# Attention inputs of the last block as tokens x features, with 512-column weights as the moving operand

## The chip, the cores and the metric

The program runs on one core of one Trainium2 chip. The metric is the device time of one execution in microseconds (us).

## What is computed

The reference runs two blocks one after the other on 256 tokens of 1024 features (the first with 16 meta tokens in front). The change lies in the second block, and there in what follows the one wide projection `proj = h @ w_in`:

```python
proj = h @ w_in[l]
(q_a, k_a, v_a, q_i, k_i, w_i, q_b, k_b, v_b, gate_a, gate_b) = jnp.split(proj, split_at, axis=-1)
q_a = apply_rope(rms_norm_2(q_a.reshape(B, S, DSA_HEADS, HEAD_DIM_2), g_q_dsa[l]), cos_h, sin_h)
k_a = apply_rope(rms_norm_2(k_a.reshape(B, S, DSA_HEADS, HEAD_DIM_2), g_k_dsa[l]), cos_h, sin_h)
...
score = jnp.einsum('bqh,bqhs->bqs', wib.astype(jnp.float32), jax.nn.relu(logits))
_, sel = lax.top_k(score, topk)
...
def rms_norm_2(x, gain):
    xf = x.astype(jnp.float32)
    y = xf * lax.rsqrt(jnp.mean(xf * xf, axis=-1, keepdims=True) + EPS)
    return (y * gain.astype(jnp.float32)).astype(x.dtype)

def apply_rope(x, cos, sin):
    x1, x2 = jnp.split(x.astype(jnp.float32), 2, axis=-1)
    return jnp.concatenate([x1 * cos - x2 * sin, x2 * cos + x1 * sin], axis=-1).astype(x.dtype)
```

The queries and keys of both attentions (4 heads of 128 features each) are normalised per token and head and rotated. The first attention (`_a`) keeps for each token the 64 keys of the best index score; the second (`_b`) is causal over the one block of 256.

## The kernel before

All matrix products are of float32 quality in three passes: a weight unit is split by ACT (ScalarE) into a rounded high part `w_hi` (L1741) and by DVE (VectorE) into the rest `w_lo` (L983, or in halves of 1024 columns by `low_half`, L1003), and PE (TensorE) forms high x high, high x low and low x high (L363 to L365) into the same PSUM bank. Weights come in units of 1 MB, 128 x 2048 numbers, through a ring of four slots. SP fetches a unit as soon as DVE is done with the slot's old one; ACT waits until PE has used up the old high part (`weights_used`, or `tile_done` at the end of a group).

Everything is held as features x tokens: the 128x128 piece of a weight is the stationary operand, and the 256 tokens of x move. The stage `w_in` has one small unit (index key and head weights) and eleven groups of 512 features, two units each: group 0 is the index queries `qi`, then `v_a`, `q_a`, `k_a`, `v_b`, `q_b`, `k_b`, and groups 7 to 10 are the gates. A group is 4 tiles x 8 input tiles x 3 passes, 96 products of 256 columns, into four of the eight banks. DVE copies the tiles out (`evict4`, L1328) and frees the banks (`tile_evicted`).

The order of every engine is written out by hand. PE runs group after group, and after each of the eight input tiles of a group a table `between` can put other work (`group`, L385):

- `turn_v`: four 128x128 transposes into bank 7 turn half of the values into tokens x features (L859).
- `qk_sums`: the squares of a head group, which ACT has made (`qk_squares`, L2020), are summed over the features by eight products with a column of ones (L651). ACT takes the root (L2025), DVE the reciprocal (L1378).
- `qk_spread`: eight products spread the reciprocals over 128 partitions (L663), twice per group, and DVE multiplies by them and by the gain (`qk_norm`, L1556).
- `qk_rotate`: a product with a signed permutation in plain float32 (L832), twice per group, and three DVE operations apply cosine and sine (`rotation`, L1509 to L1518).
- `idx_scores` (L850), `scores2` (L888, L890), `turn_p2` (L903) and `values2` (L916) are the index scores and the attention itself; the four steps of the first attention stand in groups 5 and 6, those of the second in groups 8 and 9.

All that use bank 7 wait in `bank7_free` for the last reader of it. Between them DVE finds the 64 best index scores in eight rounds of maximum and replacement for each half of the tokens (`take_best`, L1541, L1542), then writes the selection mask (`select`). `scores2` waits for it. The last group is followed by `br_dsa`.

The lines that give the shape of a product and of what stands between:

```python
ins = three_pass(ps[:, st.bank(t), 0:st.cols], u % RING, (kk * GROUP + m) * P,
                 xs[0][:, k, 0:st.cols], xs[1][:, k, 0:st.cols], k == 0, k == KT - 1)
...
def qk_jobs(name):
    return {0: [lambda: qk_sums()], 2: [lambda: qk_spread(0)], 3: [lambda: qk_spread(1)],
            4: [lambda: qk_rotate(name, 0)], 5: [lambda: qk_rotate(name, 1)]}
...
group(w_in, 3, xs, between=qk_jobs("q_a"))
group(w_in, 4, xs, between=qk_jobs("k_a"))
```

Of the kernel before, what the change touches and what calls it, by code (L numbers as in the profile page):

```python
# [24 lines left out]
ALU = mybir.AluOpType  # L25
# [42 lines left out]
N_SHIFTED = 190  # L68


class Stage:


    def __init__(self, plan, name, units, tiles, tokens, k_outer, quad_banks=False, tail=False):
# [32 lines left out]
    def evicted(self, t):  # L107

        return t - self.e_shift

# [5 lines left out]
def build(nc, w_units, mod_units, x_in, vectors, constants, tables2, out):  # L116
    ctx = ExitStack()
    with ctx:
# [27 lines left out]
        stage("w_in", "w_in", 23, 48, SEQ, False, True)  # L146
# [52 lines left out]
        v2_T = at("v2_T", 12 * KB, [P, 4, SEQ])  # L199
        qi = at("qi", 28 * KB, [P, 4, SEQ])  # L200
        gates = at("gates", 32 * KB, [P, 16, SEQ])
        work1 = at("work1", 48 * KB, [P, 4, SEQ])
        work2 = at("work2", 52 * KB, [P, 4, SEQ])
        tab = at("tab", 56 * KB, [P, 4, SEQ])
# [24 lines left out]
        def norm_part(name, offset, shape, dt=F32):  # L229
# [17 lines left out]
        eps = sb("eps", [P, 3])  # L247
# [31 lines left out]
            "scored", "max_ready", "probs_ready", "weights_ready", "p_turned", "pT_ready", "pv_done", "o_evicted",  # L279
            "idx_scored", "idx_relu", "idx_used", "sel_ready", "gate_ready",  # L280
# [18 lines left out]
        V_GROUP2 = (1, 4)  # L299
# [57 lines left out]
        def _(pe):  # L357
# [14 lines left out]
            def wait_bank(st, t, shift=0):  # L372
# [7 lines left out]
                elif st.name == "w_in" and t < st.t0 + 3 * GROUP:  # L380
                    n = st.evicted(st.t0 + GROUP)
                pe.wait_ge(S["tile_evicted"], n + shift)

            def group(st, g, xs, i=0, x_base=None, bank_busy=None, between=None):

                for half in range(2):
                    u = st.u0 + 2 * g + half + (1 if st.name == "w_in" else 0)
                    pe.wait_ge(S["lo_ready"], u + 1 + 4 * i)
                    for kk in range(4):
                        k = 4 * half + kk  # L390
                        hi_first = x_base is not None and k == 0 and st.u0 > 0
                        if hi_first:
                            pe.wait_ge(S["x_hi_ready"], x_base + 1)
                            for m in range(GROUP):
                                t = st.t0 + GROUP * g + m + (4 if st.name == "w_in" else 0)
# [6 lines left out]
                        if hi_first:  # L402
                            for m in range(GROUP):
                                t = st.t0 + GROUP * g + m + (4 if st.name == "w_in" else 0)
                                pe.matmul(ps[:, st.bank(t), 0:st.cols], w_hi[:, u % RING, m * P:m * P + P],
                                          xs[1][:, 0, 0:st.cols], start=False, stop=False)
                        for m in range(0 if not hi_first else GROUP, GROUP):
                            t = st.t0 + GROUP * g + m + (4 if st.name == "w_in" else 0)
# [403 lines left out]
            def bank7_free():  # L812

                for name, n in (("v_stored", c.now("turned")), ("rotation_read", c.now("rotated")),
                                ("head_std", c.now("head_sums")), ("normed_heads", c.now("head_spread") - 4),
                                ("o_evicted", c.now("pv_done"))):
# [3 lines left out]
            def key_and_weights():  # L820
# [6 lines left out]
                c.up("rotated")  # L827
# [26 lines left out]
            def turn_v(g, kt):  # L854

                bank7_free()
                pe.wait_ge(S["tile_evicted"], w_in.evicted(w_in.t0 + GROUP * (V_GROUP2[g] + 2)))
                for m in range(4):
                    ins = pe.transpose(ps[:, 7, m * P:(m + 1) * P], v2_T[:, m, kt * P:(kt + 1) * P], ident)  # L859
                ins.then_inc(S["turned"], 1)  # L860
                c.up("turned")
# [1399 lines left out]
```

## Time and profile before

| | |
|---|---|
| median of 3 runs | 1532.84 us (1532.22 to 1532.97) |
| profiled execution | 1531.38 us |
| its span | 1529.5 us |
| PE / weight loads busy | 1474.2 us (96%) / 1443.6 us (94%) |
| DVE / ACT busy | 1065.0 us (70%) / 680.7 us (45%) |
| mean granted clock of PE | 0.994 |
| read from HBM | 266.73 MB, 175 GB/s |

The span is what the profile shows of the execution; the execution's own time holds about 2 us more. The busy time of PE counts overlapping products once, so 96% says that something was always in the array, not that it ran at its best rate. How fast products follow each other is read from their starting times in the timeline.

### The profile page before, as it was taken

How to read it: one execution, taken by the hardware profiler on the slowest of the kernel's cores; microseconds unless marked ns; L12 is line 12 of the kernel's file. 1: busy time of each engine (PE TensorE's matmuls, PEld its weight loads, DVE VectorE, ACT ScalarE, POOL GpSimd, SP SyncE). 2: the span in 40 equal slices, each digit the busy share in tenths (PEclk: the TensorE clock that was granted, in tenths of full speed). 3: DMA queues.
4: the chain of work that ended last, by engine and by line, in shares of the span. 5: the costliest groups of instructions: out<-in, count | busy, mean ns of one | idle time of the engine just before them, and what ended most of it. 6: DMA issues, size and time to landing. Idle time of an engine off the chain costs nothing. (4 is left out here: it accounts for less than half of the span.)

```text
span 1529.5 us, 29328 instructions
## 1 busy us (share of the span) xinstructions
PE 1474.2 (96%) x12027; PEld 1443.6 (94%) x12027; DVE 1065.0 (70%) x1443; ACT 680.7 (45%) x809; POOL 28.9 (2%) x58
## 2 busy tenths in 40 slices
PE   5999999999999999999999979999999999999999
PEld 4999999999999999999988879999898989999999
DVE  5666878776667876677867676668877665776653
ACT  5443344354443454433545555443432535454441
POOL 0000100000000000000000000001000000000000
PEclk9999999999999999999999989999999999999999
DMA  7545745436447555457332135558343234454550
GB/s 295 188 166 191 262 179 193 165 105 244 174 165 251 217 193 184 173 196 286 141 131 107 60 138 193 201 187 302 149 142 134 84 117 179 173 188 170 176 209 29
DMA packets 41677, 269.14 MB, mean 176 GB/s; under 512 B 4672, under 2 KB 5824, under 8 KB 12272
## 3 DMA queue, kind: packets, MB, share of 16 engines
q1 hardware_dynamic: 33120, 240.31, 43.6%
q0 software_dynamic: 7312, 26.44, 4.9%
q8 instruction: 71, 1.16, 0.3%
q10 hardware_dynamic: 1152, 1.05, 0.2%
q14 instruction: 22, 0.18, 0.0%
HBM read 266.73 MB, written 1.05 MB: 175 GB/s over the span
## 5 line engine op out<-in xcount | busy, mean ns | idle before, releaser
L363 PE MATMUL ps<-x_hi,w_hi 128*128 128x272 f32 (+2 forms) x2488 | 725.1, 291 | 29.6 <-DVE w_lo L983 16.5
L364 PE MATMUL ps<-x_lo,w_hi 128*128 128x272 f32 (+2 forms) x2488 | 708.6, 285 | 0.0
L365 PE MATMUL ps<-x_hi,w_lo 128*128 128x272 f32 (+2 forms) x2488 | 708.5, 285 | 0.0
L1741 ACT ACTIVATE w_hi<-raw_weights 128x2048 fp32r<-128x2048 f32 x222 | 423.5, 1912 | 362.7 <-PE ps L365 362.5
L983 DVE TENSOR_TENSOR w_lo<-raw_weights,w_hi 128x2048 fp32r<-128x2048 f32 x196 | 447.1, 2290 | 167.3 <-ACT w_hi L1741 166.7
L363 PEld LDWEIGHTS ps<-x_hi,w_hi 128*128 128x128 f32 x2488 | 472.6, 190 | 37.8 <-DVE w_lo L983 16.5
L364 PEld LDWEIGHTS ps<-x_lo,w_hi 128*128 128x128 f32 x2488 | 473.0, 190 | 2.8 <-issue 2.4
L365 PEld LDWEIGHTS ps<-x_hi,w_lo 128*128 128x128 f32 x2488 | 472.5, 190 | 0.0
L363 PE MATMUL ps<-a_hi,w_hi 128*128 128x272 f32 x592 | 169.6, 286 | 0.0
L364 PE MATMUL ps<-a_lo,w_hi 128*128 128x272 f32 x592 | 169.6, 286 | 0.0
L365 PE MATMUL ps<-a_hi,w_lo 128*128 128x272 f32 x592 | 169.6, 286 | 0.0
L363 PE MATMUL ps<-a_hi_s,w_hi 128*128 128x256 f32 x416 | 116.1, 279 | 1.3 <-DVE o L1384 0.8
L364 PE MATMUL ps<-a_lo_s,w_hi 128*128 128x256 f32 x416 | 115.0, 276 | 0.0
L365 PE MATMUL ps<-a_hi_s,w_lo 128*128 128x256 f32 x416 | 115.0, 276 | 0.0
L363 PEld LDWEIGHTS ps<-a_hi,w_hi 128*128 128x128 f32 x592 | 111.5, 188 | 0.0
L364 PEld LDWEIGHTS ps<-a_lo,w_hi 128*128 128x128 f32 x592 | 111.5, 188 | 0.0
L365 PEld LDWEIGHTS ps<-a_hi,w_lo 128*128 128x128 f32 x592 | 111.5, 188 | 0.0
L1768 ACT ACTIVATE pair_a<-pair_a 128x544 f32<-128x544 f32 (+1 forms) x44 | 28.7, 653 | 168.5 <-DVE pair_a L1026 168.5
L363 PEld LDWEIGHTS ps<-a_hi_s,w_hi 128*128 128x128 f32 x416 | 78.2, 188 | 1.8 <-DVE o L1384 1.0
L1003 DVE TENSOR_TENSOR w_lo<-raw_weights,w_hi 128x1024 fp32r<-128x1024 f32 (+1 forms) x71 | 77.9, 1111 | 2.4 <-ACT w_hi L1741 1.9
L364 PEld LDWEIGHTS ps<-a_lo_s,w_hi 128*128 128x128 f32 x416 | 78.2, 188 | 0.1
L365 PEld LDWEIGHTS ps<-a_hi_s,w_lo 128*128 128x128 f32 x416 | 78.2, 188 | 0.0
(247 smaller groups left out, 1375.2 us busy)
## 6 DMA issues: line engine op xcount, KB each, us to landing
raw_weights<-w_units SPq DMA_DIRECT2D x228, 1024.0 KB, 4.9
mod_w<-mod_units POOLq DMA_DIRECT2D x48, 512.0 KB, 5.3
h<-x_in SPq DMA_DIRECT2D x1, 1088.0 KB, 5.5
out<-h ACTq DMA_DIRECT2D x8, 128.0 KB, 1.9
tab<-tables POOLq DMA_DIRECT2D x1, 512.0 KB, 10.0
tab<-constants POOLq DMA_DIRECT2D x1, 272.0 KB, 3.1
con<-constants POOLq DMA_DIRECT2D x2, 128.0 KB, 6.6
f<-constants POOLq DMA_DIRECT2D x1, 136.0 KB, 7.0
```

Of the source, the lines that this page charges most:

```text
L363: pe.matmul(dst, wh, hi, start=start, stop=False)
L364: pe.matmul(dst, wh, lo, start=False, stop=False)
L365: return pe.matmul(dst, wl, hi, start=False, stop=stop)
L983: dve.tensor_tensor(w_lo[:, u % RING, :], raw[:, u % RING, :], w_hi[:, u % RING, :].bitcast(F32), ALU.subtract).then_inc(S["lo_ready"], 1)
L1003: ins = dve.tensor_tensor(w_lo[:, u % RING, cols], raw[:, u % RING, cols], w_hi[:, u % RING, cols].bitcast(F32), ALU.subtract)
L1741: act.activation(w_hi[:, u % RING, :], raw[:, u % RING, :], ACT.Copy).then_inc(S["hi_ready"], 1)
L1768: act.activation(pair_a[:, :, 0:T], pair_a[:, :, 0:T], ACT.Silu).then_inc(S["silu_done"], 1)
```

## The change

Six of the eleven groups (`v_a`, `q_a`, `k_a`, `v_b`, `q_b`, `k_b`) are computed as tokens x features. The new function `rows(j, ...)` takes the 128x128 piece of x (128 features, half of the tokens) as the stationary operand and 512 weight columns as the moving one. One product fills a bank; a group takes two banks, one for each half of the tokens, and pairs of banks alternate (0, 1 and 2, 3).

- Values are stored by ACT straight from PSUM; `turn_v` goes.
- The sum of squares of a token and head is a row sum, which ACT takes while squaring (`row_squares`, four instructions of 128 columns for each half); `qk_sums` goes, `qk_spread` too.
- Queries are not multiplied by their reciprocal root. It goes, with the factor 1/sqrt(128), as a per-token scale into the exponential (`q_col`). Keys are scaled by ACT (`row_scale`), four instructions for each half.
- The rotation swaps the halves of a head by addressing (`row_rope`: two products of 512 columns and two sums of 256 for each half); `qk_rotate` goes. Cosine and sine, times the gain, are needed as tokens x features: DVE scales the tables four times (`scale_tables`), PE turns them in four steps (`turn_tab`), ACT stores them.
- Queries and keys are turned back by PE (`turn_rows`, four transposes each, eight times) and stored by ACT (`store_rows`).
- A bank is free for the group after next when its reader is done: the values' copy, the queries' products, or the keys' scaling (`rows_free`). The gates of group 7 take the banks of `q_b` and `k_b`.

What follows is the core of the diff; the new stream of jobs is complete for PE and for DVE up to the second attention.

```diff
@@ Stage
+            elif name == "w_in" and FIRST_ROW <= n < FIRST_ROW + 2 * ROW_GROUPS:
+                if (n - FIRST_ROW) % 2 == 1:
+                    plan["used"].append(("rows_done", n - FIRST_ROW + 1))
+                else:
+                    plan["mid"] += 1
+                    plan["used"].append(("weights_used", plan["mid"]))
+                continue
@@ PE
+        ROW_BANKS = ((0, 1), (2, 3))
+        ROW_V, ROW_QK = (0, 3), (1, 2, 4, 5)
...
                 elif st.name == "w_in" and t < st.t0 + 3 * GROUP:
-                    n = st.evicted(st.t0 + GROUP)
+                    m = t - st.t0 - 2 * GROUP
+                    rows_free(ROW_GROUPS - 2 + m // 2, m % 2)
+                    return
...
+            def rows_free(j, qt):
+
+                if j in ROW_V:
+                    pe.wait_ge(S["v_stored"], 6 + 2 * ROW_V.index(j) + qt + 1)
+                    return
+                n = ROW_QK.index(j)
+                if n % 2 == 0:
+                    pe.wait_ge(S["row_products"], 2 * n + qt + 1)
+                else:
+                    pe.wait_ge(S["row_scaled"], n - 1 + qt + 1)
...
+            def rows(j, between):
+
+                for half in range(2):
+                    u = w_in.u0 + FIRST_ROW + 2 * j + half
+                    pe.wait_ge(S["lo_ready"], u + 1)
+                    for kk in range(4):
+                        k = 4 * half + kk
+                        wh, wl = (w[:, u % RING, 4 * P * kk:4 * P * (kk + 1)] for w in (w_hi, w_lo))
+                        for qt in range(2):
...
+                            dst = ps[:, ROW_BANKS[j % 2][qt], :]
+                            xh, xl = (x[:, k, qt * P:(qt + 1) * P] for x in (x_hi, x_lo))
+                            pe.matmul(dst, xh, wh, start=k == 0, stop=False)
+                            pe.matmul(dst, xl, wh, start=False, stop=False)
+                            ins = pe.matmul(dst, xh, wl, start=False, stop=k == KT - 1)
...
+            rows(0, {
+                0: [lambda: rotate_qi(0)], 1: [lambda: rotate_qi(1)], 2: [lambda: turn_tab(0)],
+                3: [lambda: idx_scores(0)], 4: [lambda: turn_tab(1)], 6: [lambda: idx_scores(1)]})
+            rows(1, {0: [lambda: turn_tab(2)], 1: [lambda: turn_tab(3)], 2: [lambda: idx_scores(2)]})
+            rows(2, {4: [lambda: turn_rows(0, 0)], 6: [lambda: turn_rows(0, 1)]})
+            rows(3, {6: [lambda: turn_rows(1, 0)], 7: [lambda: turn_rows(1, 1)]})
+            rows(4, {
+                1: [lambda: scores2(0)],
+                3: [lambda: scores2(1), lambda: turn_p2(0)], 4: [lambda: values2(0)],
+                5: [lambda: scores2(2), lambda: turn_p2(1)], 6: [lambda: values2(1)],
+                7: [lambda: scores2(3), lambda: turn_p2(2)]})
+            rows(5, {
+                0: [lambda: values2(2)], 1: [lambda: turn_p2(3)], 2: [lambda: values2(3)],
+                4: [lambda: turn_rows(2, 0)], 6: [lambda: turn_rows(2, 1)]})
+            group(w_in, 7, xs, between={5: [lambda: turn_rows(3, 0)], 7: [lambda: turn_rows(3, 1)]})
@@ DVE
+            def row_rope(n, qt):
...
+                dve.tensor_tensor(straight, src, cos, ALU.mult).then_inc(S["vec_chain"], 1)
+                dve.tensor_tensor(crossed, src, sin, ALU.mult).then_inc(S["row_products"], 1)
...
+                dve.tensor_tensor(dst[:, :, 0:half], straight[:, :, 0:half], crossed[:, :, half:P], ALU.subtract)
+                dve.tensor_tensor(dst[:, :, half:P], straight[:, :, half:P], crossed[:, :, 0:half], ALU.add)\
+                   .then_inc(S["row_roped"], 1)
...
             idx_add(2)
             take_best(0, TOPK // 8 - 3)
...
+            row_rope(0, 0)
+            low_half()
+            row_rope(0, 1)
+            low_half()
+            row_roots(0)
             take_best(0, 3)
+            low_half()
+            low_half()
+            take_best(1, 1)
+
+            low_half()
+            take_best(1, 2)
+            row_roots(1)
+            low_half()
+            take_best(1, 2)
+            row_rope(1, 0)
+            low_half()
+            row_rope(1, 1)
+            low_half()
+            take_best(1, 3)
             for qt in range(2):
                 select(qt)
@@ ACT
+                for m in range(HEADS2):
+                    ins = act.activation(f[:, 4 + m, qt * P:(qt + 1) * P], ps[:, ROW_BANKS[j % 2][qt], m * P:(m + 1) * P], ACT.Square,
+                                         accum_out=row_sum[:, 4 * qt + m:4 * qt + m + 1])
...
+                    ins = act.activation(row_k[:, qt, m, :], ps[:, ROW_BANKS[j % 2][qt], m * P:(m + 1) * P], ACT.Identity,
+                                         scale=head_col[:, 8 + 4 * qt + m:9 + 4 * qt + m])
```

The order of instructions is shown at two places. The first is PE at a group's start. Before, the last tile of the first input tile of group 6 (`k_b`) and what stands behind it (`con,f` is the sum of the squares of `q_b`, 128x1 a column of ones):

```order
L363 MATMUL ps<-x_hi,w_hi 128x256 [waits tile_evicted]
L364 MATMUL ps<-x_lo,w_hi 128x256
L365 MATMUL ps<-x_hi,w_lo 128x256
L651 MATMUL ps<-con,f 128x1 [waits normed_heads,o_evicted,head_std,head_sq,rotation_read,v_stored]
L651 MATMUL ps<-con,f 128x1 x7
L363 MATMUL ps<-x_hi,w_hi 128x256
```

In the changed kernel, PE where the row group `k_b` ends and group 7, the first gates, begins:

```order
L930 MATMUL ps<-w_hi,x_hi 128x512
L931 MATMUL ps<-w_hi,x_lo 128x512
L932 MATMUL ps<-w_lo,x_hi 128x512
L385 MATMUL ps<-x_hi,w_hi 128x256 [waits row_products,lo_ready]
L386 MATMUL ps<-x_lo,w_hi 128x256
L387 MATMUL ps<-x_hi,w_lo 128x256
L385 MATMUL ps<-x_hi,w_hi 128x256 [waits row_products]
L386 MATMUL ps<-x_lo,w_hi 128x256
L387 MATMUL ps<-x_hi,w_lo 128x256
L385 MATMUL ps<-x_hi,w_hi 128x256 [waits row_scaled]
L386 MATMUL ps<-x_lo,w_hi 128x256
L387 MATMUL ps<-x_hi,w_lo 128x256
```

The sums between the products are gone; the third tile of group 7 now waits for ACT's scaling of the keys whose product ended just before it.

The second place is ACT around the same keys. Before:

```order
L1741 ACTIVATE w_hi<-raw_weights 128x2048 [waits weights_used,raw_loaded1]
L1741 ACTIVATE w_hi<-raw_weights 128x2048 [waits tile_done,raw_loaded2]
L2020 ACTIVATE f<-k_b 128x4x256 [waits tile_evicted]
L2025 ACTIVATE head_col<-ps,eps 128x8 [waits head_columns,head_sums]
L1741 ACTIVATE w_hi<-raw_weights 128x2048 [waits weights_used,raw_loaded3]
```

In the changed kernel:

```order
L2099 ACTIVATE f,row_sum<-ps 128x128 [waits rows_done]
L2099 ACTIVATE f,row_sum<-ps 128x128 x3
L2099 ACTIVATE f,row_sum<-ps 128x128 [waits rows_done]
L2099 ACTIVATE f,row_sum<-ps 128x128 x3
L2108 ACTIVATE head_col<-row_sum,eps 128x8 [waits head_columns,row_sums]
L2118 ACTIVATE row_k<-ps,head_col 128x128 [waits row_products,head_columns]
L2118 ACTIVATE row_k<-ps,head_col 128x128 x3
L2118 ACTIVATE row_k<-ps,head_col 128x128 [waits row_products,head_columns]
L2118 ACTIVATE row_k<-ps,head_col 128x128 x3
L1817 ACTIVATE w_hi<-raw_weights 128x2048 [waits rows_done,raw_loaded2]
L2126 ACTIVATE k_b<-ps 128x4x128 [waits rows_turned]
```

Two instructions on the keys became sixteen narrow ones, a root and two stores, and the next weight unit's split stands behind them.

## Rows read from the trace of the kernel before

**Rows 1.** the page: busy time of the engines over the whole span
```profile
PE 1474.2 (96%) x12027; PEld 1443.6 (94%) x12027; DVE 1065.0 (70%) x1443; ACT 680.7 (45%) x809; POOL 28.9 (2%) x58
```

**Rows 2.** timeline of PE (start us, us, ...): the first product of br_dsa
```profile
1291.43 0.47 PE L363 MATMUL ps<-o_hi,w_hi 128*128 128x256 f32 x1 [2.30 <-DVE gates L1328]
```

**Rows 3.** stretches: us, PE, PEld, DVE, ACT, POOL busy, granted clock, DMA
```profile
1121.64:1291.43 169.79, 160.18 (x1279) 150.39 (x1277) 119.45 (x209) 71.91 (x93) 0.00 (x0) 0.99 0.37 129
...
1172.00:1175.00 3.00, 1.94 (x17) 1.97 (x18) 2.97 (x6) 0.92 (x1) 0.00 (x0) 1.00 0.33 49
1175.00:1178.00 3.00, 3.00 (x17) 3.00 (x18) 2.27 (x6) 0.27 (x1) 0.00 (x0) 0.58 0.90 325
1178.00:1181.00 3.00, 3.00 (x24) 3.00 (x24) 0.56 (x1) 0.00 (x0) 0.00 (x0) 0.85 0.83 325
```

**Rows 4.** timeline of PE: two unbroken runs of products, 28 and 82 steps
```profile
1109.40 0.28 PE L364 MATMUL ps<-x_lo,w_hi 128*128 128x256 f32 x1
...
1112.69 0.28 PE L365 MATMUL ps<-x_hi,w_lo 128*128 128x256 f32 x1
...
1113.59 0.28 PE L364 MATMUL ps<-x_lo,w_hi 128*128 128x256 f32 x1
...
1122.88 0.28 PE L365 MATMUL ps<-x_hi,w_lo 128*128 128x256 f32 x1
```

**Rows 5.** timeline of PE: turning, index scores, sum, rotation, spread, and products after them
```profile
1141.09 0.60 PE L859 MATMUL ps<-con,v_T 128*128 128x128 f32 x4
...
1141.65 0.28 PE L364 MATMUL ps<-x_lo,w_hi 128*128 128x256 f32 x1
...
1143.00 1.13 PE L850 MATMUL ps<-ki,qi 64*128 64x256 f32 x8
...
1173.07 1.92 PE L651 MATMUL ps<-con,f 128*128 128x1 f32 x16 [1.21 <-ACT f L2020]
...
1175.05 0.28 PE L364 MATMUL ps<-x_lo,w_hi 128*128 128x256 f32 x1
...
1186.20 1.02 PE L832 MATMUL ps<-k_a,con 128*128 128x512 f32 x2
...
1187.18 0.28 PE L364 MATMUL ps<-x_lo,w_hi 128*128 128x256 f32 x1
...
1221.80 1.05 PE L663 MATMUL ps<-con,head_col 128*128 128x128 f32 x8
...
1222.82 0.28 PE L364 MATMUL ps<-x_lo,w_hi 128*128 128x256 f32 x1
```

**Rows 6.** groups of DVE, 1145.2 to 1195 us (busy us, mean ns | idle before)
```profile
L1003 DVE TENSOR_TENSOR w_lo<-raw_weights,w_hi 128x1024 fp32r<-128x1024 f32 x9 | 10.6, 1210 | 0.1
L1541 DVE MAX8 top<-score 128x8 f32<-128x128 f32 (+1 forms) x16 | 5.8, 360 | 0.4
L1542 DVE MATCH_REPLACE8 score<-top,score 128x128 f32<-128x128 f32 (+1 forms) x16 | 5.5, 342 | 0.0
L1509 DVE TENSOR_TENSOR work<-ps,tab 128x512 f32<-128x512 f32 x4 | 2.8, 692 | 1.3 <-PE ps L832 1.1
...
L1542 DVE MATCH_VALUE_LOAD score<-top,score 128x8 f32 x16 | 1.5, 92 | 0.5
```

**Rows 7.** timeline of DVE: the first search for the best eight
```profile
1147.33 0.29 DVE L1541 MAX8 top<-score 128x8 f32<-128x128 f32 x1
```

**Rows 8.** timeline of ACT: two exponentials of 128 columns with their row sums
```profile
1198.23 0.37 ACT L1892 ACTIVATE pair_a<-ps,small 128x128 f32<-128x128 f32 x1 [2.09 <-DVE small L1339]
...
1198.59 0.36 ACT L1892 ACTIVATE pair_a<-ps,small 128x128 f32<-128x128 f32 x1
```

**Rows 9.** groups of ACT, 1121 to 1291 us
```profile
L2025 ACT ACT_TABLE_LOAD x1 | 1.3, 1283 | 0.0
...
L2025 ACT ACTIVATE head_col<-ps,eps 128x8 f32<-128x8 f32 x4 | 1.1, 267 | 7.2 <-PE ps L651 7.2
```

**Rows 10.** waits of PE, 1121.2 to 1292 us (total us, times, longest us)
```profile
PE ps L651 <- ACT f L2020: 2.3, 2, 1.2
```

More of the change, by code:

```diff
@@ L109, in evicted, with tile @@
         return t - self.e_shift
+    def tile(self, g):
+        if self.name != "w_in":
+            return self.t0 + GROUP * g
+        return self.t0 + GROUP * (g + 1 if g == 0 else g + 1 - ROW_GROUPS)
     def bank(self, t):
@@ L954, in _ @@
-            group(w_in, 7, xs, between=qk_jobs("k_b"))
+            rows(0, {
[4 more added lines that the diff above has]
+            rows(3, {6: [lambda: turn_rows(1, 0)], 7: [lambda: turn_rows(1, 1)]})
@@ new lines, in store_rows, with store_tab @@
+            def store_rows(n, qt):
+                dst = qkv2[("q_a", "k_a", "q_b", "k_b")[n]]
+                act.wait_ge(S["rows_turned"], 2 * n + qt + 1)
+                act.activation(dst[:, :, qt * P:(qt + 1) * P], ps[:, 7, :].rearrange("p (a n) -> p a n", a=HEADS2),
+                               ACT.Copy).then_inc(S["rows_stored"], 1)
+            def store_tab(n):
+                act.wait_ge(S["tab_turned"], n + 1)
+                act.activation(row_tab[:, n, :, :, :], ps[:, 7, :].rearrange("p (a b n) -> p a b n", a=2, b=2),
+                               ACT.Copy).then_inc(S["tab_stored"], 1)
@@ L2063, in _ @@
             split()
+            store_tab(0)
             relu(0)
+            store_tab(1)
             split()
             relu(1)
[L2068 removed]
             store_v2(0)
             store_v2(1)
+            store_tab(2)
+            store_tab(3)
+            split()
             relu(2)
             split()
[L2074 to L2080 removed]
+            row_squares(0, 0)
+            row_squares(0, 1)
+            row_std(0)
+            split()
+            store_rows(0, 0)
+            split()
+            store_rows(0, 1)
+            row_squares(1, 0)
+            row_squares(1, 1)
+            row_std(1)
+            row_scale(1, 0)
+            row_scale(1, 1)
+            split()
+            store_rows(1, 0)
+            split()
+            store_rows(1, 1)
             store_v2(2)
@@ L2100, in _ @@
             split()
+            store_rows(2, 0)
             split()
-            qk_squares(6, "k_b")
-            qk_std(3)
+            store_rows(2, 1)
+            row_squares(3, 0)
+            row_squares(3, 1)
+            row_std(3)
+            row_scale(3, 0)
+            row_scale(3, 1)
             split()
+            store_rows(3, 0)
+            split()
+            store_rows(3, 1)
             split()
```

239 lines of the change are left out of this document (121 added, 118 removed).

## The prediction, on record before the changed kernel ran

> **What bounds the kernel now.** I read the page first: PE is busy for 96% of the span, DVE for 70% and ACT for 45% [rows 1]. So PE sets the time, and a microsecond taken from its queue counts wherever its next work is ready. Then I cut out the stretch that the change rewrites: from the first product of group 1 at 1121.64 us to the first product of br_dsa at 1291.43 us, 169.8 us, of which PE is idle 169.8 - 160.2 = 9.6 us [rows 2, 3]. What lies ahead of it and behind it runs the same instructions. A 256-column product is listed with about 280 ns, but that is latency; what counts is the distance of the starts. In two unbroken runs 28 steps take 3.29 us and 82 steps take 9.29 us, so 117.5 and 113.3 ns each [rows 4]. Both distances come back through the whole stretch, and I take their middle, 115.5 ns.
>
> **The row products.** Six groups of 96 products of 256 columns become six of 48 of 512, 576 against 288. Nothing in the trace moves 512 rounded columns. From below, at the full clock of 2.4 GHz (granted clock 1.00 around the runs) 512 columns need 213.3 ns; from above, two old steps are 231 ns and nothing is gained. The 256-column steps lie 6.7 and 10.8 ns over their columns' 106.7 ns; I take one such surcharge, 8.7 ns, so 222 ns: 288 x (231 - 222) = **2.6 us gained**, between 0 and 5.1. The Trainium skill ("TensorE: Matmul & The Clock Gate", Back-to-back issue gap) gives 2.5 ns over the columns for an isolated warm product, 215.8 ns here; by it the term would be 4.4 us and the time 1.8 us lower. The 256-column rows don't agree with 2.5 ns, they show 6.7 to 10.8, with a weight load before each product.
>
> **What leaves PE's queue.** The cost of a job is the time from its start to the second product behind it, less one step of 115.5 ns, since the first product behind a job takes longer too [rows 5]:
> - turning the values: 1141.65 - 1141.09 less a step, 0.445 us, four times: 1.8 us;
> - sums of squares: 1175.05 - 1173.07 less a step, 1.865 us, four times: 7.5 us;
> - rotation: 1187.18 - 1186.20 less a step, 0.865 us, eight times: 6.9 us;
> - spreads: 1222.82 - 1221.80 less a step, 0.905 us, eight times: 7.2 us.
>
> Together **23.4 us gained**, none of it under other work, for PE is the engine they stand on.
>
> **What enters it.** Four turnings of the tables and eight of rows, each four 128x128 transposes like those of the values: 12 x 0.445 = **5.4 us lost**. Turning has its like in the rows, so its bounds are narrow.
>
> **What moves to DVE and ACT.** DVE loses the copies out of PSUM, the norms and six operations of rotation per group and gets eight of `row_rope`; the table scaling (four operations of 512 columns, 0.69 us each by the nearest row [rows 6]) falls where DVE waits for the split of unit 5, before the stretch. ACT gets sixteen narrow instructions for a head group where one wide one was. They cost nothing until PE waits for them. PE does so at these places.
>
> (a) The mask. In the changed order DVE has, from the first search for best scores at 1147.33 us (what is ahead of it keeps its time) [rows 7] to the end of `select`: 16 searches, 5.8 + 5.5 + 1.5 us busy and 0.9 idle before them, 13.7 us; eight halves of a split, 10.7 / 9 each, 9.5 us; four `row_rope`, two products of 0.69 and two half-wide sums of 0.35, 8.4 us; two reciprocals and four short mask operations, about 1.6 us at the replacement's 0.34 [rows 6]. That is 33.2 us without a gap, until 1180.5 us. PE, unhindered, reaches the first `scores2` after 204 row products, 45.3 us, two rotations of `qi`, three index scores of 1.2 us (one takes 1.13 and delays the next product by 0.1) and eight turnings: 1121.64 + 45.3 + 1.7 + 3.6 + 3.6 = 1175.9 us [rows 5]. So it loses **4.6 us** up to there, part of it at the turning of `k_a`.
> (b) `values2(3)`. ACT has the squares of `q_b`, a table load of 1.28 us and the root ahead of the copy of the turned probabilities that PE needs. A square of 128 columns with its row sum goes at 0.36 us from start to start, like the exponential [rows 8], so eight take 2.9 us; with the load, the root of 0.27 [rows 9] and two copies of some 0.5, it is 5.4 us after `values2(2)`. PE has two input tiles (2.7 us) and a turning (0.45) meanwhile: **2.3 us**.
> (c) The start of group 7. Its third tile writes the bank of `k_b`'s first half. Counted from the last product of that half, ACT and DVE need 0.15 + 2.9 (squares) + 0.27 (root) + 0.2 (reciprocal) + 1.2 (four scalings, estimated at 0.28 from one to the next: the exponential's 0.36 without the reading of its sum) and some 0.2 between the engines, 4.9 us. PE has three row products and six gate products, 1.4 us. It waits **3.5 us**, and another **0.75 us** for the second half, 1.1 us behind the first less three products.
> (d) 2.3 us before br_dsa stay [rows 2], and 0.4 us of another gate eviction.
>
> The sum is 13.9 us, and each of nine waits slows the first product behind it by 0.1: **14.8 us**. What they replace: 9.6 us idle, 12 waits that hide another 0.26 us each in the last product's end and the restart (3.1 us), and the clock. From 1175 to 1181 us the granted clock is 0.58 and 0.85, between the levels of 2.4 and 1.2 GHz, right behind the wait and the sums of `k_a` in which PE was busy for 1.94 of 3 us; that took 0.42 x 3 + 0.15 x 3 = 1.7 us [rows 3]. The largest of the old waits that go are those for the squares [rows 10]. Together **14.4 us**, so the waits cancel to 0.4 us.
>
> **Sum.** 2.6 + 23.4 - 5.4 - 0.4 = 20.2 us. The profiled execution took 1531.38 us (span 1529.5), 1.5 us under the median of the runs; it would go to 1511.2 us, and the median from 1532.84 to **1512.6 us**.
>
> **Rivals.**
> 1. *The new waits are dearer than counted, and the clock falls in them* (chance 0.18). The wait of (c), 3.5 us, is longer than the 1.21 us ahead of the sums behind which the clock fell [rows 3, 5]; one such fall costs 1.7 us, two 3.4. And if DVE's operations with a broadcast table take 10% longer than the plain ones of [rows 6], the whole list of (a) shifts, 3.3 us. Against it: other waits in the stretch brought no fall, and (c) is one wait followed by dense work. Time: 1512.6 + 1.7 to 1512.6 + 1.7 + 1.7 + 3.3, so 1514.3 to 1519.3 us. The Trainium skill (the same page, "Why this matters for your kernels") says that idle gaps between bursts of products return PE to the lower clock; it speaks for this rival. The trace agrees once: the fall to 0.58.
> 2. *Fewer waits* (0.12). If ACT squares and scales faster out of PSUM than the exponential suggests and DVE is on time, (a) vanishes and the row step is near 213 ns: 1512.6 - 4.6 - 2.5 = 1505.5 us. For it speaks only that each list was laid end to end; against it that `select` has 4.6 us to make up.
> 3. *Slower: 512 moving columns don't keep the rate* (0.03). The only product of 512 columns in the stretch is the rotation, at 0.865 us [rows 5], four times 216 ns: plain float32 is slow there, and no row shows that the rounded form keeps one column per cycle at that width. At half the rate a product takes 427 ns, 288 x 0.205 = 59 us more, 1572 us. It decides from 222 + 20200 / 288 = 292 ns on.
> 4. *The trade comes to nothing* (0.01): the turnings and their waits would have to cost 20 us more than in (a) to (c). Time 1532.8 us. Turnings at their price [rows 5] can't; it needs waits of 35 us in the stretch.
>
> **How the numbers follow.** The forecast itself, 1509 to 1516 us, has 0.66. The range takes in most of rival 1 and nearly all of rival 2: 1506 to 1520 us. About 0.2% (3 us) is what can be told from no change; rivals 1 and 2 and the forecast are all faster by more: faster 0.96, same 0.01, slower 0.03.
>
> **What would show it.** Row products start 222 ns apart, 288 of them; no L651, L663 or 512-column rotation behind those of `qi`; twelve groups of four transposes. From the first row product to br_dsa 149.6 us in place of 169.8. PE waits for DVE's mask or its turning rows before the first attention, about 4.6 us in all, for ACT's copy before `values2(3)`, and 4.3 us at the third and fourth tile of group 7 for ACT's scaling. The rest of the program, before and behind, keeps its time within 1 us. I am wrong if the row step is over 230 ns, if PE idles over 20 us in the stretch, or if the gates' groups 8 to 10 lose time that they didn't lose before.

## The result: 1517.0 us, and the profile after

| | before | after |
|---|---|---|
| median | 1532.95 us (1532.22 to 1535.43, 6 runs) | 1517.0 us (1511.95 to 1524.61, 6 runs) |
| ratio | | 0.9888 (95%: 0.987 to 0.9906) |
| profiled execution, its span | 1531.38, 1529.5 us | 1511.95, 1510.1 us |
| group 1 to br_dsa | 169.79 us, PE idle 9.6 | 150.25 us, PE idle 10.4 |

The changed kernel is 16 us faster; forecast were 20.2. Its runs scatter over 12 us, and the profiled one is the fastest of the six.

The page and PE's arrival at br_dsa, to be held against [rows 1, 2]:

```profile
PE 1457.1 (96%) x11627; PEld 1415.9 (94%) x11627; DVE 1053.0 (70%) x1436; ACT 697.8 (46%) x897; POOL 29.0 (2%) x58
```
```profile
1272.70 0.35 PE L385 MATMUL ps<-o_hi,w_hi 128*128 128x256 f32 x1 [2.31 <-DVE gates L1377]
```

PE has 17.1 us less work and is as full as before. The 2.3 us ahead of br_dsa are the same as in [rows 2]. The stretches, with the columns of [rows 3] (the first is the rewritten one, the others are the start of group 7):

```profile
1122.45:1272.70 150.25, 139.81 (x879) 120.90 (x877) 105.96 (x197) 88.30 (x181) 0.00 (x0) 0.99 0.41 146
...
1212.00:1215.00 3.00, 0.73 (x7) 0.53 (x5) 1.09 (x2) 2.70 (x17) 0.00 (x0) 1.00 0.43 175
1215.00:1218.00 3.00, 2.39 (x10) 2.09 (x11) 2.26 (x5) 3.00 (x7) 0.00 (x0) 0.61 0.46 139
1218.00:1221.00 3.00, 3.00 (x24) 3.00 (x23) 2.75 (x4) 0.13 (x1) 0.00 (x0) 0.82 0.50 210
```

The rewritten stretch went from 169.79 to 150.25 us, 19.5 us less. The rest of the span kept its time: 1121.64 and 1122.45 us ahead of it, 238.07 and 237.40 us behind. At 1215 us the granted clock falls between the levels of 2.4 and 1.2 GHz, right after PE was busy for 0.73 of 3 us; (1 - 0.61) x 3 + (1 - 0.82) x 3 = 1.7 us are lost. It is the fall that rival 1 spoke of, at the place it named.

What PE waited for in the stretch (total us, times, longest), in place of [rows 10]:

```profile
PE ps L385 <- ACT row_k L2118: 2.9, 2, 2.6
PE ps L385 <- DVE gates L1377: 2.7, 2, 2.3
PE ps L952 <- issue: 1.8, 1, 1.8
PE ps L980 <- ACT pT L2156: 1.5, 1, 1.5
PE ps L907 <- DVE row_out L1639: 1.2, 1, 1.2
PE ps L898 <- issue: 0.4, 1, 0.4
```

All places (a) to (d) are there. The wait put down to "issue" is the one for the mask, as the timelines of DVE and PE show together: the first search for best scores, the end of the mask, PE's last row product ahead of it and the first `scores2`.

```profile
1149.94 0.29 DVE L1594 MAX8 top<-score 128x8 f32<-128x128 f32 x1
...
1181.81 0.43 DVE L1602 TENSOR_TENSOR sel<-score,mask 128x256 bf16<-128x256 f32 x1
```
```profile
1180.16 0.40 PE L932 MATMUL ps<-w_lo,x_hi 128*128 128x512 f32 x1
1182.34 0.46 PE L952 MATMUL ps<-k_a,q_a 128*128 128x128 f32 x2 [1.78 <-issue]
```

From search to mask DVE needs 1181.81 + 0.43 - 1149.94 = 32.3 us; 33.2 were listed. It starts 1149.94 - 1122.45 = 27.5 us into the stretch, before at 25.7 [rows 3, 7].

The new row products, two ends of a run of 58 steps (answering to [rows 4]):

```profile
1145.76 0.40 PE L931 MATMUL ps<-w_hi,x_lo 128*128 128x512 f32 x1
...
1159.05 0.40 PE L932 MATMUL ps<-w_lo,x_hi 128*128 128x512 f32 x1
```

13.29 us by 58 is **229 ns**, where I took 222. Last, ACT ahead of `values2(3)` and ahead of group 7: the first and last square of `q_b`, the table load, the root and the copy PE waits for; then the first square of `k_b`, its root and the scalings.

```profile
1198.69 0.27 ACT L2099 ACTIVATE f<-ps 128x128 f32<-128x128 f32 x1
...
1200.44 0.33 ACT L2099 ACTIVATE f<-ps 128x128 f32<-128x128 f32 x1
...
1200.88 1.28 ACT L2108 ACT_TABLE_LOAD   x1
1202.17 0.30 ACT L2108 ACTIVATE head_col<-row_sum,eps 128x8 f32<-128x8 f32 x1
1202.38 0.58 ACT L2156 ACTIVATE pT<-ps 128x512 f32<-128x512 f32 x1
...
1211.37 0.28 ACT L2099 ACTIVATE f<-ps 128x128 f32<-128x128 f32 x1
...
1213.58 0.30 ACT L2108 ACTIVATE head_col<-row_sum,eps 128x8 f32<-128x8 f32 x1
1214.15 2.18 ACT L2118 ACTIVATE row_k<-ps,head_col 128x128 f32<-128x128 f32 x8 [0.27 <-DVE head_col L1615]
```

From the first of the eight squares to the last are 1.75 us, seven distances of 0.25 us and not 0.36: the square with its row sum is cheaper than the exponential of [rows 8].

### The profile page after: what moved, and what is told of

It reads as the page before. It is cut to its first block and busy times, and to the rows that moved or that the text cites. A ratio compares the mean times of both kernels' runs of the same rounds, so it can differ in the third digit from the quotient of the medians.

```text
span 1510.1 us, 28569 instructions
## 1 busy us (share of the span) xinstructions
PE 1457.1 (96%) x11627; PEld 1415.9 (94%) x11627; DVE 1053.0 (70%) x1436; ACT 697.8 (46%) x897; POOL 29.0 (2%) x58
## 5 line engine op out<-in xcount | busy, mean ns | idle before, releaser
L385 PE MATMUL ps<-x_hi,w_hi 128*128 128x272 f32 (+2 forms) x2296 | 664.9, 290 | 29.0 <-DVE w_lo L1031 16.6
L386 PE MATMUL ps<-x_lo,w_hi 128*128 128x272 f32 (+2 forms) x2296 | 654.5, 285 | 0.0
L387 PE MATMUL ps<-x_hi,w_lo 128*128 128x272 f32 (+2 forms) x2296 | 654.3, 285 | 0.0
L385 PEld LDWEIGHTS ps<-x_hi,w_hi 128*128 128x128 f32 x2296 | 436.1, 190 | 33.2 <-DVE w_lo L1031 16.6
L386 PEld LDWEIGHTS ps<-x_lo,w_hi 128*128 128x128 f32 x2296 | 436.3, 190 | 0.5
L387 PEld LDWEIGHTS ps<-x_hi,w_lo 128*128 128x128 f32 x2296 | 436.1, 190 | 0.0
```

The lines of the kernel that those rows point to most:

```text
L385: pe.matmul(dst, wh, hi, start=start, stop=False)
L386: pe.matmul(dst, wh, lo, start=False, stop=False)
L387: return pe.matmul(dst, wl, hi, start=False, stop=stop)
```

## The experiments

Ten kernels ran beside the kernel before, in three sessions: 1536.24 us (11 runs) for the first four, 1537.8 us (17 runs) for the next four, 1536.71 us (13 runs) for the last two. The kernel before takes 1530 to 1543 us in them; the runs of the first table lay at its lower end.

Four questions: is the gain the work taken from PE, at its prices (the old jobs put back, apart and together, the turnings doubled)? Is it the width of the products? Which of the new waits cost what (three moves)? And where does the scatter come from (both kernels unaltered)?

**The changed kernel again.** No edit.

> The changed kernel once more, for the spread of its executions (1511.95 to 1524.61 us in six, while the kernel before keeps within 3.2 us). Theory A, the clock: the waits at the start of group 7 and elsewhere drop PE to 1.2 GHz in some executions; then the slow executions have a lower mean granted clock than the fast ones (0.3 points for 5 us) and a slow trace shows stretches at 0.5 beside the waits. Theory B, late weights: in some executions a unit of weights arrives late for ACT; the mean clock is no lower, and a slow trace shows PE waiting for w_lo in the stretch from 1122 to 1273 us.

Measured: 1516.84 us (1510.87 to 1520.49, 5 runs), ratio 0.9863 (0.9844 to 0.9883). Its profile has the same waits, a stretch of 152.1 us, and a span of 1518.6 us, 8.5 us more than the first. Only 1.9 us of that is in the stretch; 5.2 us come ahead of it, where both kernels run the same instructions. The 1.9 us are nearly all one more fall of the clock, right behind the wait for the mask; (1 - 0.65) x 3 + (1 - 0.79) x 3 = 1.7 us are lost:

```profile
1188.00:1191.00 3.00, 3.00 (x13) 2.40 (x12) 2.29 (x6) 1.90 (x5) 0.00 (x0) 0.65 0.01 3
1191.00:1194.00 3.00, 3.00 (x15) 2.34 (x14) 0.06 (x1) 0.89 (x1) 0.00 (x0) 0.79 0.00 0
```

So theory A holds for that part. Theory B finds nothing in the stretch, where PE waits nowhere for `w_lo`. Neither explains the larger part.

**Group 7's third and fourth tile in other banks.** They go to banks 4 and 5, so that they need not wait for the keys' scaling:

```diff
     def bank(self, t):
+        if self.name == "w_in" and t - self.t0 in (10, 11):
+            return t - self.t0 - 6
...
                 elif st.name == "w_in" and t < st.t0 + 3 * GROUP:
                     m = t - st.t0 - 2 * GROUP
+                    if m >= 2:
+                        pe.wait_ge(S["probs_ready"], 2 * c.now("scored"))
+                        return
```

> Group 7's third and fourth tile go to banks 4 and 5, free after the fourth scores, instead of waiting for the scaling of the keys k_b. My reading: the 2.9 us of wait for ACT's row_k go, and the fall of the clock behind them (1.7 us): 3.5 to 5 us less than the changed kernel. If the spread comes from that wait (theory A), it narrows to the 3 us of the kernel before; if it comes from late weights (theory B), it stays. Rival: the wait only moves, to the scores of the second attention, and nothing is gained.

Measured: 1508.28 us (1505.34 to 1514.3, 6 runs), ratio 0.9811 (0.9796 to 0.9826). The stretch:

```profile
1127.52:1272.75 145.23, 137.46 (x878) 119.08 (x877) 105.96 (x197) 88.30 (x181) 0.00 (x0) 1.00 0.43 151
```

5.0 us less than 150.25, with no wait for `row_k` (2.9 us) and no fall of the clock in group 7 (1.7 us). With the clock, the wait of (c) cost more than its own length. It was a matter of which banks the tiles use, no price of computing keys as rows. The median is 8.6 us under that of the changed kernel in the same session, more than the 3.5 to 5 us expected; the trace carries 5.0 of them, and the rest stays open. Nor is that wait where the scatter comes from: without it the six runs still lie 9 us apart, and those of the kernel before up to 12 us in one session.

**Products of 512 columns as two of 256.**

```diff
-                            pe.matmul(dst, xh, wh, start=k == 0, stop=False)
-                            pe.matmul(dst, xl, wh, start=False, stop=False)
-                            ins = pe.matmul(dst, xh, wl, start=False, stop=k == KT - 1)
+                            for h in (slice(0, SEQ), slice(SEQ, 2 * SEQ)):
+                                pe.matmul(dst[:, h], xh, wh[:, h], start=k == 0 and h.start == 0, stop=False)
+                                pe.matmul(dst[:, h], xl, wh[:, h], start=False, stop=False)
+                                ins = pe.matmul(dst[:, h], xh, wl[:, h], start=False, stop=k == KT - 1 and h.start > 0)
```

> The row products as two of 256 columns each, 576 in place of 288, each with its own weight load; all else as in the changed kernel. The starts of the 512-column products in the changed kernel's trace lie 229 ns apart, so with 113 to 118 ns for 256 columns the stretch grows by 288 x (231 - 229) = 0 to 2 us. By the page's 215.8 ns for 512 columns it would be 4.4 us. If it costs more than 5 us, the wide product is worth more than the trace's starting times say.

Measured: 1517.86 us (1512.61 to 1521.84, 6 runs), ratio 0.9877 (0.9856 to 0.9899). The stretch, and br_dsa at its end:

```profile
1128.57:1279.34 150.77, 140.82 (x1166) 135.72 (x1165) 105.97 (x197) 88.34 (x181) 0.00 (x0) 0.99 0.41 145
```
```profile
1279.34 0.36 PE L385 MATMUL ps<-o_hi,w_hi 128*128 128x256 f32 x1 [2.52 <-DVE gates L1378]
```

150.8 us, 0.5 us over the 512-column form; PE is idle for 9.95 us in place of 10.4, so its own work grew by 1.0 us. So the width, from which the change has its name, is worth about a microsecond of the 19.5; the rest comes from what the layout makes needless.

**Two more waits taken.** On top of the other banks: ACT copies the turned probabilities between the two halves of `q_b`'s squares, ahead of the root and its table load, and one half split of DVE goes from before the last searches to behind the mask.

```diff
             row_rope(1, 1)
-            low_half()
             take_best(1, 3)
             for qt in range(2):
                 select(qt)
+            low_half()
@@ ACT
             row_squares(2, 0)
-            row_squares(2, 1)
-            row_std(2)
             store_p2(3)
+            row_squares(2, 1)
             store_o2(3)
+            row_std(2)
```

> As e2, and two more waits taken away by order alone: ACT copies the turned probabilities of the fourth step between the two squares of q_b, ahead of the root and its table load; DVE makes the second half of the low part of unit 12 behind the selection mask instead of ahead of it. My reading: 1.5 us at the fourth values and 1.2 us of the 3.4 us ahead of the first scores go, so 2.5 to 3 us less than e2, 6 to 8 less than the changed kernel. Rival: DVE or ACT is late elsewhere instead and only e2's part stays.

Measured: 1504.71 us (1503.7 to 1510.29, 5 runs), ratio 0.9804 (0.9786 to 0.9823); stretch 142.51 us, 2.7 less than with the banks alone. Two of its waits:

```profile
PE ps L912 <- DVE row_out L1644: 1.2, 1, 1.2
...
PE ps L957 <- issue: 0.7, 1, 0.7
```

The wait for `pT` (1.5 us) is gone and the one for the mask is 0.7 in place of 1.8: 2.6 us, as the stretch has it.

**The wait ahead of br_dsa.** One more move:

```diff
-            split_to(u0 + 26)
+            split_to(u0 + 25)
             for which in range(2):
...
+            split_to(u0 + 26)
             store(10, gates[:, 12:16, :])
```

> The version of e4_three with one more move: DVE forms the rest of the attention's output (o2_lo, three operations of about 0.3 to 0.7 us) one half split earlier, so that the last tile of gates before br_dsa is not queued behind it. Theory (the 2.3 us ahead of br_dsa are DVE's queue: the copy of the gates stands behind a half split of 1.2 us and o2_lo): the wait before the first product of br_dsa falls from 2.3 us to about 1 us and with it, perhaps, the fall of the clock behind it (1.7 us): 1.4 to 3 us less than e4_three, so 1502 to 1503.5 us. Rival (DVE is in arrears there in any order, since it is the sum of its work that is late): the wait moves to the next place that needs DVE and the time stays within 0.5 us of e4_three's 1504.7 us.

Measured: 1503.31 us (1501.93 to 1509.25, 6 runs), ratio 0.9784 (0.976 to 0.9807). DVE there, and PE's first product of br_dsa:

```profile
1259.10 2.35 DVE L1767 TENSOR_TENSOR o_lo<-f,o_hi 128x1024 fp32r<-128x1024 f32 x2
1263.09 2.29 DVE L1036 TENSOR_TENSOR w_lo<-raw_weights,w_hi 128x2048 fp32r<-128x2048 f32 x1 [1.64 <-ACT w_hi L1823]
1266.10 1.40 DVE L1382 COPY gates<-ps 128x512 f32<-128x512 f32 x2 [0.72 <-PE ps L389]
```
```profile
1267.64 0.36 PE L387 MATMUL ps<-o_hi,w_hi 128*128 128x256 f32 x1 [0.94 <-DVE gates L1382]
```

The copy of the gates now waits for PE, and no longer stands behind DVE's own 2.35 us of `o_lo`. The wait is 0.94 in place of 2.3 us and the stretch 141.20 us, 1.3 us less: the cause is shown. The clock, which fell to 0.74 and 0.69 right behind this wait in the version before, does not fall here (1.00 from 1264 to 1273 us); that lies behind the stretch, and what follows to the end takes 238.2 us there and 237.4 here. (The expectation had `o_lo` as three operations of 0.3 to 0.7 us; it is two of 1.2.) The medians of the two versions are 1.4 us apart, but were taken in different sessions, and their ranges overlap; the trace carries this step. This version is the fastest, 34.5 us under the kernel before in its session, and beats both kernels.

**The old jobs back, as idle work.** The products of `qk_sums`, `qk_spread` and `qk_rotate` run again, on constants and into bank 7; no one reads them. (One call of `qk_spread` is four products, which the profile lists as eight records; the kernel's description says eight.)

```diff
+            def idle_sums():
+                bank7_free()
+                for n in range(8):
+                    pe.matmul(ps[:, 7, n:n + 1], con[:, P:2 * P], ones[:, 0:1], start=True, stop=True)
...
+            rows(2, {0: [idle_sums], 2: [idle_spread], 3: [idle_spread], 4: [lambda: turn_rows(0, 0), idle_rotate],
+                     5: [idle_rotate], 6: [lambda: turn_rows(0, 1)]})
```

and likewise in `rows(3)`, `rows(5)` and group 7.

> The changed kernel with the products of the removed jobs put back on PE as idle work into bank 7, on constants, at the places where they used to stand: four times the eight sums, eight times the four spreads, eight times the one plain float32 rotation of 512 columns. Nothing reads them. By the prices read from the trace of before (1.865, 0.905 and 0.865 us) that is 7.5 + 7.2 + 6.9 = 21.6 us on PE's queue. Theory (the gain is work taken from PE at these prices; a part of the new waits is only there because PE comes earlier): the waits ahead of the mask (3 us) and of the last values (1.5 us) are filled, those of group 7 (2.9 us) and before br_dsa (2.3 us) stay, so +17 us over the changed kernel, 15 to 19, and the lead over the kernel before is nearly gone. Rival (the gain comes from the shape of the products or from waits, and the jobs were partly hidden): +8 us or less. In the trace each kind of job costs its old price within 0.1 us.

Measured: 1540.17 us (1535.65 to 1543.48, 10 runs), ratio 1.002 (1.0001 to 1.004): 23 us over the changed kernel, outside my 15 to 19. The stretch is 173.80 us, 23.55 more than 150.25. PE's waits show a part of why:

```profile
PE ps L923 <- ACT q_b L2145: 1.0, 1, 1.0
PE ps L923 <- ACT q_a L2145: 0.9, 1, 0.9
PE ps L923 <- ACT k_b L2145: 0.9, 1, 0.9
PE ps L919 <- ACT q_b L2145: 0.9, 1, 0.9
```

Idle products behind a turning wait until ACT has stored the turned rows out of bank 7: 3.6 us that my placing added. And in the windows from 1227 us the clock falls, for longer than anywhere in the changed kernel:

```profile
1227.00:1230.00 3.00, 0.86 (x3) 0.72 (x3) 2.17 (x4) 2.70 (x13) 0.00 (x0) 0.82 0.00 0
1230.00:1233.00 3.00, 2.98 (x15) 2.83 (x14) 2.22 (x4) 1.92 (x2) 0.00 (x0) 0.50 0.89 319
```

It stays at 0.50 until 1239 us and costs 5.1 us. PE is busy for 0.86 of 3 us in the window in which it begins, and the wait there is the 2.6 us for `row_k` that ends at 1229.1 us. The same account as below fits this version too: 23.55 us longer, 0.9 us less idle (9.6 in place of 10.4), 3.4 us more lost by the clock, so 23.55 + 0.9 - 3.4 = 21.0 us of work. Over the forecast are thus the placing and the clock, not the jobs' price.

**The old jobs, none behind a turning.** Where a rotation or spread stood right behind a turning it now stands after another input tile.

> As e6_old_jobs (the old jobs' products back as idle work in bank 7), but none directly behind a turning of rows: in e6_old_jobs four of them waited 0.9 to 1.0 us each for ACT to store the turned rows out of bank 7, 3.7 us in all, and the clock fell behind the last of these waits (to 0.50 for 12 us). Theory (the old jobs are worth 21.6 us on PE and fill 4.8 us of the new waits; the rest of e6_old_jobs' 23.55 us in the stretch was the placing): the four waits are gone, the stretch from the first row product to br_dsa takes 150.25 + 21.6 - 4.8 = 167 us, 166 to 168.5, and the time is 1533 to 1535.5 us, some 17 us over the changed kernel. Rival (the jobs cost more than their price, by slowing what stands around them): the stretch stays over 170 us.

Measured: 1530.54 us (1526.45 to 1537.65, 10 runs), ratio 0.997 (0.9951 to 0.9988). The stretch:

```profile
1122.12:1289.77 167.65, 162.38 (x1023) 140.59 (x1021) 105.97 (x197) 88.09 (x181) 0.00 (x0) 0.98 0.37 131
```

167.65 us; 167 were expected. PE is idle for 5.3 us, 5.2 less than in the changed kernel: the waits for the mask, the rows and `pT` are filled, and 0.7 us of the one for `row_k`. The clock falls once (from 1227 us, 3.4 us). (The expectation reads the long fall of the last version wrongly: it lasts 10 us and begins at the end of the wait for `row_k`; the last wait for bank 7 comes 19 us later.) One job of each kind, with the second product behind it:

```profile
1153.49 1.84 PE L914 MATMUL ps<-con 128*128 128x1 f32 x16
...
1155.51 0.39 PE L945 MATMUL ps<-w_hi,x_lo 128*128 128x512 f32 x1
...
1158.04 1.05 PE L919 MATMUL ps<-con 128*128 128x128 f32 x8
...
1159.16 0.39 PE L945 MATMUL ps<-w_hi,x_lo 128*128 128x512 f32 x1
...
1164.44 1.02 PE L923 MATMUL ps<-con 128*128 128x512 f32 x2
...
1165.52 0.39 PE L945 MATMUL ps<-w_hi,x_lo 128*128 128x512 f32 x1
```

Less a step of 0.229 us these are 1.79, 0.89 and 0.85 us, where 1.865, 0.905 and 0.865 were read from [rows 5]; times 4, 8 and 8 they make 21.1 us (21.6 forecast). From the whole stretch it is 17.4 + 5.2 (filled) - 1.7 (3.4 of clock less the 1.7 that the changed kernel lost too) = 20.9 us. The two agree.

The median missed: 1533 to 1535.5 us were expected, some 17 us over the changed kernel. It is 11.7 us over the changed kernel of the same session (1518.81 us, below) and 6.2 us under the kernel before. The profiled executions of the two differ by 11.4 us as well, and there one sees where: 17.3 us more in the stretch, 1.1 more behind it, but 6.9 us less ahead of it (1122.12 and 1129.01 us), where both run the same instructions. So the price of the jobs rests on the stretches; the medians alone would not show it.

**Every turning of rows twice.**

```diff
-                for m in range(HEADS2):
+                for m in 2 * list(range(HEADS2)):
                     ins = pe.transpose(ps[:, 7, m * P:(m + 1) * P], row_out[:, qt, m, :], ident)
```

> The changed kernel with each of the eight turnings of rows done twice over into the same place: 32 more 128x128 transposes, nothing else. By the price of a turning in the trace of before (0.445 us for four) 3.6 us more on PE. Two of the eight stand ahead of waits for the mask and two ahead of the wait of group 7's scaled keys, where PE's delay doesn't fill that wait since the keys' chain starts behind PE's own products. Theory (turnings stand on PE's path at 0.445 us, the first four partly filled by the wait for the mask): +1.8 to +3.6 us. Rival (a turning costs more than its columns, because it waits for its rows or delays the store that others wait for): over 4.5 us.

Measured: 1517.67 us (1514.7 to 1517.95, 4 runs), ratio 0.9873 (0.9847 to 0.99), which by the times alone is no difference from the changed kernel. The stretch is clearer:

```profile
1121.07:1273.78 152.71, 143.72 (x910) 125.09 (x909) 105.95 (x197) 88.16 (x181) 0.00 (x0) 0.99 0.39 144
```

2.5 us more than 150.25, and 9.0 us idle in place of 10.4: PE's own work grew by some 3.9 us, for 3.6 priced. Taken singly, a doubled turning with the next product takes 1.107 us and a simple one 0.667 us (starts of the turning and of the second product behind it), 0.44 us more. The rival's 4.5 us are not reached.

**Both kernels once more**, for other profiled executions.

> The kernel before once more, for another profiled execution of it. Two things are open: whether the distance of 256-column products is again one of two values (113.3 or 117.8 ns) that a whole stage keeps, and whether it falls on the same stages. Theory (the value is a matter of the single execution): some stages show another value than in the first profile, and the span differs from 1529.5 us by as much as their steps make it, up to 10 us. Rival (the value belongs to the kernel's code at that place): the same values on the same stages, span within 1 us.

Measured: 1535.71 us, span 1533.9.

```profile
1123.20:1295.73 172.53, 162.76 (x1278) 152.97 (x1277) 119.44 (x209) 71.93 (x93) 0.00 (x0) 0.97 0.35 127
...
1179.00:1182.00 3.00, 3.00 (x16) 3.00 (x15) 1.57 (x4) 0.00 (x0) 0.00 (x0) 0.50 0.74 273
1236.00:1239.00 3.00, 3.00 (x19) 3.00 (x20) 3.00 (x5) 0.27 (x1) 0.00 (x0) 0.66 0.95 333
```

The waits are those of the first profile within 0.2 us, but the stretch is 2.7 us longer: the clock falls at three places of it (from 1158, 1179 and 1236 us, 5.1 us lost), where the first profile had one (1.7 us). The 256-column steps kept 113.3 ns from 930 to 1080 us as in the first profile; from 1321 to 1340 us they are 117.8 ns here and 113.7 there. So the same instructions at the same place can have either value.

> The changed kernel unaltered, for the comparison with e9_old_jobs_apart on the same chip, and for a third profiled execution: stretch 150 to 152.5 us, the waits of the first two profiles within 0.5 us each, time 1514 to 1519 us. The distance of 512-column row products is 229 ns again if it is a property of the product, and it moves by about 9 ns (twice the 4.5 ns between the two values of the 256-column step) if it is subject to the same two states.

Measured: 1518.81 us (1513.7 to 1521.97, 4 runs), ratio 0.988 (0.9845 to 0.9916); span 1519.0 us. The changed stretch:

```profile
1129.01:1279.39 150.38, 139.61 (x879) 120.77 (x877) 105.97 (x197) 88.24 (x181) 0.00 (x0) 0.99 0.40 145
```

The stretch repeats to 0.13 us, with the same waits. The 8.9 us by which the span is longer lie outside: 6.6 us ahead, 2.2 behind. Two unbroken runs of the same products show most of it, in the first profile of the changed kernel and in this one:

```profile
959.84 0.28 PE L387 MATMUL ps<-x_hi,w_lo 128*128 128x256 f32 x1
...
971.96 0.28 PE L386 MATMUL ps<-x_lo,w_hi 128*128 128x256 f32 x1
```
```profile
959.75 0.28 PE L385 MATMUL ps<-x_hi,w_hi 128*128 128x256 f32 x1
...
971.89 0.28 PE L386 MATMUL ps<-x_lo,w_hi 128*128 128x256 f32 x1
```

107 steps of 113.3 ns there, 103 of 117.9 ns here. The 4.6 ns hold from 930 to 1080 us; over the 1326 products of these 150 us that is 6 us. The larger value holds there in three of the twelve profiles. The 512-column step is 229.4 to 230.1 ns in all nine profiles that have it (the mean of the steps below 240 ns in the whole stretch). It doesn't share the two values.

## Why the prediction was right, and where its terms were off

The forecast was 1512.6 us (range 1506 to 1520), measured are 1517.0. The size and the place held: 19.5 us of the stretch for 20.2, and nothing elsewhere that the change made. With the terms as measured below (row products 0.5, sums, spreads and rotations 21.0, values' turnings 1.8 as priced, all new turnings 5.5 lost, and the waits' account 1.4 gained, which is the forecast's 14.4 less 10.4 idle, 1.7 of clock and 0.9 at the products behind the waits) the sum is 19.2 us.

- **The row products: mis-sized.** The step is 229 ns, not 222, a nanosecond below the 230 named as a sign of being wrong, and [rows 4]'s surcharge of one step (8.7 ns) is no guide to it: 512 columns take 16 ns over their 213.3. By the sum's own 231 that leaves 0.5 us in place of 2.6. What it replaced varies: in the profile of before, 58 steps from 1144.29 to 1151.12 us are 117.8 ns apart, and with such steps it would be 288 x (235.6 - 229) = 1.9 us. The halves cost PE 1.0 us in the trace, between the two. By the Trainium skill ("TensorE: Matmul & The Clock Gate", Back-to-back issue gap) an isolated product would take 2.5 ns over its columns, 215.8 ns; these products, with a weight load before each, don't agree.
- **What leaves PE's queue: right.** Sums, spreads and rotations: 21.6 us priced, 20.9 to 21.1 put back. The values' turnings were not tried apart.
- **What enters it: right.** 3.6 us priced for eight turnings, 3.5 to 3.9 when doubled. The four turnings of the tables were not tried apart.
- **(a) the mask: right in kind, 3.0 us (1.8 and 1.2 at the turning of `k_a`) for 4.6.** DVE's list was 0.9 us too long but began 1.8 us later than assumed; PE came later by more. 204 row products at 229 ns alone are 1.4 us of it.
- **(b) the turned probabilities: 1.5 us for 2.3**, and **(c) group 7: 2.9 us for 4.25.** The main cause of both: eight squares take 2.0 us and not 2.9. The exponential of [rows 8] was the wrong neighbour for the square out of PSUM.
- **(d) 2.3 and 0.4 us: right**, and the first was removable.
- **Rival 1, in part.** The waits were cheaper than in the forecast, yet the clock fell behind (c), which the forecast had put at nothing. With the 1.7 us of the clock and 10.4 us idle in place of 13.9, the waits' account ended 1.8 us better than forecast, which covers most of the 2.1 us missing in the products. That the sum came within a microsecond owes something to errors that cancel. The 3.1 us said to be hidden in the ends of the old waits were an estimate that no run tried.
- **Rivals 2 to 4 fell.** Of rival 2 one condition came true, the faster squares, but the wait for the mask stayed at 3.0 us and the step is not near 213 ns. The step is far under the 292 ns of rival 3, and nothing cost 20 us.
- **The median is 4.4 us over the forecast, and the stretch does not show why.** I took the profiled execution of before to be 1.5 us under the median, as three runs said; in the later sessions that median is 1536 to 1538 us. The first changed profile was lucky too, 5 us under the median of its six. In the three sessions that ran both kernels their medians lie 15.9, 19.4 and 17.9 us apart. Between executions the clock's falls and the 256-column step change, over stages that the change doesn't touch: in the twelve profiles the time ahead of the stretch, the same instructions in all, is 1121.1 to 1129.0 us. That the median's miss is this scatter is likely, not shown. The forecast said that the rest keeps its time within 1 us; that holds for what the code does there, but not for single executions.

## What to carry to other kernels

Computing a result in the layout in which its norm and rotation work along a row can pay by the small matrix products that it makes needless, even if each main product gets hardly cheaper: price these products by the distance to the second product behind them, and put them back as idle work to test it. Then look at the first tiles of the next group: a bank that still waits for its reader stopped PE for 2.9 us and cost 5 with the clock, and two free banks took it all away. Read short differences from the stretch that was changed, since the whole time scatters by more than they are.

## What the runs showed of the hardware

- **A 256-column product follows the last at 113.3 or at 117.8 ns**, and one value can hold for 150 us of dense work; the same instructions had one in some executions and the other in others (6 us over that stage). The 512-column step has no such pair, 229.4 to 230.1 ns. What decides the value was not tried and stays open.
- **The clock falls differ from execution to execution of one kernel.** In one profile of the kernel before it fell once in the stretch (1.7 us), in the other three times (5.1 us). Behind the 2.3 to 2.5 us ahead of br_dsa it fell in nine of the eleven profiles that have this wait, and not where the wait was 0.94 us. The fall in group 7 went with its wait, too: it stands in all seven profiles with that wait and in none of the three of the changed layout without it. The Trainium skill ("TensorE: Matmul & The Clock Gate", Why this matters for your kernels) says that idle gaps between bursts of products, if they are long enough, return PE to the lower clock; nine profiles have the fall behind the wait ahead of br_dsa, two with the same wait keep the full clock, and why is open.
- **A square with its row sum is faster than an exponential with its row sum**: 0.25 against 0.36 us for 128 columns out of PSUM, one start to the next.
